# One more of the sixteen expert groups computed ahead: where the spilled products and the early picks stand, and the fourth one-hot buffer as one tensor

## What is computed

```python
def peer_ffn(xn, wq, keys, u_tab, v_tab):            # per token: 8 heads, 16 experts each
    q = (xb @ wq).reshape(C, PEER_HEADS, 2, PEER_DK_HALF)
    s = jnp.einsum('chpd,hpnd->chpn', q, keys)
    sv, si = lax.top_k(s, K)                         # K = 16, for both halves of the key
    cand = sv[:, :, 0, :, None] + sv[:, :, 1, None, :]
    cidx = si[:, :, 0, :, None] * N_KEYS + si[:, :, 1, None, :]
    top_s, sel = lax.top_k(cand.reshape(C, PEER_HEADS, K * K), K)
    eidx = jnp.take_along_axis(cidx.reshape(...), sel, axis=-1)
    g = jax.nn.softmax(top_s, axis=-1)
    act = jax.nn.gelu(jnp.einsum('chkd,cd->chk', u_tab[eidx], xb))
    return jnp.einsum('chk,chkd->cd', g * act, v_tab[eidx])
...
    h = h + peer_ffn(rmsnorm(h, g_ffn_norm[l]), peer_wq[l], peer_keys[l], peer_u[l], peer_v[l])
```

## Time and profile before

| | |
|---|---|
| Time, median of 3 runs | 2046.16 us (2044.97 to 2049.4) |
| Time of the profiled execution | 2044.4 us |
| Its span | 2042.6 us |
| PE busy | 1989.7 us (97%) |
| DVE busy | 1513.5 us (74%) |
| POOL busy | 1076.8 us (53%) |
| ACT busy | 980.6 us (48%) |
| DMA | 446.78 MB, mean 219 GB/s |
| Three scatter tiles | 424.8 to 707.7 us |
| Expert stage | 707.7 to about 1452 us |

### The profile page before, as it was taken

One profiled execution on the slowest core, in us unless ns is written; L12 is line 12 of the kernel. 1 busy time (PEld: TensorE's weight loads), 2 busy tenths in 40 slices (PEclk: granted clock), 3 DMA queues, 4 the chain that ended last, 5 costly groups with the idle time before them and its releaser, 6 DMA issues.

```text
span 2042.6 us, 31709 instructions
## 1 busy us (share of the span) xinstructions
PE 1989.7 (97%) x11783; PEld 1775.4 (87%) x11783; DVE 1513.5 (74%) x2883; ACT 980.6 (48%) x1805; POOL 1076.8 (53%) x646
## 2 busy tenths in 40 slices
PE   9999999999889999999999999999999999999998
PEld 8746889999889999999999999999877787877787
DVE  6237548989899858989999999988686635067763
ACT  4337433356779833333433333334556652255643
POOL 3213456875445767776777777674335444411242
PEclk9999999999899999999999999999999999999999
DMA  5330224767678999999999999997312222210021
GB/s 206 81 101 12 73 93 158 260 212 266 225 255 294 344 354 377 403 393 372 392 385 381 401 387 413 365 399 254 119 68 93 84 93 103 95 40 32 21 83 62
DMA packets 155144, 446.78 MB, mean 219 GB/s; under 512 B 14960, under 2 KB 60912, under 8 KB 152816
## 3 DMA queue, kind: packets, MB, share of 16 engines
q1 hardware_dynamic: 108912, 276.96, 38.4%
q0 software_dynamic: 46080, 167.79, 21.6%
HBM read 405.39 MB, written 39.31 MB: 218 GB/s over the span
## 4 chain that ended last, share of the span: by engine, by line
PE 77%; DVE 13%; DMA 3%; issue 3%; ACT 2%; POOL 2%; SPq 0%; DVEq 0%; ACTq 0%
PE bank L528 16%; PE bank L529 16%; PE bank L530 16%; PE bank L934 3%; PE bank L936 3%; PE bank L935 3%; PE bank L915 2%; PE bank L1156 2%; DVE fetched L2384 1%; PE bank L703 1%; DVE hots L2341 1%; DVE wide L2404 1%; DMA fetched<-in_v_rows,extra_rows 1%; PE wide L1179 1%; PE wide L1167 1%
## 5 line engine op out<-in xcount | busy, mean ns | idle before, releaser
L2725 POOL TENSOR_TENSOR wl<-wraw,wh 128x1024 fp32r<-128x1024 f32 x272 | 670.9, 2471 | 616.1 <-ACT wh L1347 613.9
L1347 ACT CAST wh<-wraw 128x1024 fp32r<-128x1024 f32 x360 | 374.1, 1045 | 150.5 <-PE bank L530 120.2
L528 PE MATMUL bank<-WTH,wh 128*128 128x352 f32 x1024 | 333.9, 326 | 7.6 <-issue 7.4
L529 PE MATMUL bank<-WTL,wh 128*128 128x352 f32 x1024 | 332.1, 324 | 0.0
L530 PE MATMUL bank<-WTH,wl 128*128 128x352 f32 x1024 | 332.0, 324 | 0.0
L528 PE MATMUL bank<-AXH,wh 128*128 128x352 f32 (+1 forms) x832 | 299.3, 360 | 6.9 <-issue 3.4
L530 PE MATMUL bank<-AXH,wl 128*128 128x352 f32 (+1 forms) x832 | 295.6, 355 | 0.0
L529 PE MATMUL bank<-AXL,wh 128*128 128x352 f32 (+1 forms) x832 | 295.5, 355 | 0.0
L934 PE MATMUL bank<-AXH,wh 128*128 128x352 f32 x576 | 193.7, 336 | 10.6 <-issue 10.6
L528 PEld LDWEIGHTS bank<-WTH,wh 128*128 128x128 f32 x1024 | 192.1, 188 | 12.7 <-issue 12.2
L2848 POOL DMA_INDIRECT fetched<-in_u_rows,diag x128 | 140.0, 1094 | 108.5 <-DVE fetched L2384 87.7
(11 more groups left out here) (557 smaller groups left out, 4116.2 us busy)
## 6 DMA issues: line engine op xcount, KB each, us to landing
wraw<-in_wstream SPq DMA_DIRECT2D x360, 512.0 KB
g_scratch<-gs SPq DMA_DIRECT2D x11, 2048.0 KB
gr<-g_scratch SPq DMA_DIRECT2D x15, 1408.0 KB
a_scratch<-tmp SPq DMA_DIRECT2D x72, 176.0 KB
tmp<-a_scratch SPq DMA_DIRECT2D x44, 176.0 KB
sq<-a_scratch SPq DMA_DIRECT2D x28, 176.0 KB
shifted<-hc_scratch SPq DMA_DIRECT2D x12, 270.0 KB, 4.8
h<-in_hT SPq DMA_DIRECT2D x8, 264.0 KB, 6.1
```

Of the source, the lines that this page charges most:

```text
L528: pe.matmul(o, w1, x1, start=n == 0, stop=False)
L529: pe.matmul(o, w1, x2, start=False, stop=False)
L1347: act.copy(wh[n % NSPLIT][:, :], wraw[n % NRAW][:, :]).then_inc(*w_hi.tell(n))
L2725: return pool.tensor_tensor(lo, src, hi.bitcast(F32), ALU.subtract)
```

## The change

One more group is spilled, so that its 8 U products leave the expert stage for the scatter tiles. The three tiles get 18, 20 and 12 spilled products for 15, 14 and 13, and 8, 12 and 26 early picks for 12, 12 and 22. The places of the six groups that stay dense are chosen anew. The two `sq` buffers become the halves of one tensor, so that the fourth one-hot pair is written by one DVE instruction in place of two. The weight stream is laid out in the new order.

```diff
-SPILLED = 9
-DENSE_AT = (0, 2, 4, 7, 9, 11, 14)
+SPILLED = 10
+DENSE_AT = (0, 2, 5, 8, 11, 14)
...
-    sq = [sb(ctx, f"sq{i}", [128, T]) for i in range(2)]
+    both_sq = sb(ctx, "sq", [128, 2, T])
+    sq = [both_sq[:, i, :] for i in range(2)]
...
-    hots.append((*(x[:, 0:512].rearrange("p (i c) -> p i c", i=4) for x in sq), None))
+    hot3 = both_sq[:, :, 0:512].rearrange("p a (i c) -> p a i c", i=4)
+    hots.append((hot3[:, 0, :, :], hot3[:, 1, :, :], hot3))
...
-                base, count = ((30, 15), (45, 14), (59, 13))[tt - 1]
+                base, count = ((30, 18), (48, 20), (68, 12))[tt - 1]
...
-                while picks < (10, 22, 34)[tt - 1] + (12, 12, 22)[tt - 1] * now // whole:
+                while picks < (10, 18, 30)[tt - 1] + (8, 12, 26)[tt - 1] * now // whole:
...
-                if q % 4 == 3:
-                    for x in range(2):
-                        dve.tensor_tensor(hots[3][x], iota_psum.unsqueeze(1).to_broadcast([128, 4, 128]),
-                                          places[:, x].to_broadcast([128, 4, 128]),
-                                          ALU.is_equal).then_inc(*hot.tell((q, x), q))
...
+                dve.tensor_tensor(hots[q % 4][2], iota_psum.unsqueeze(1).unsqueeze(1).to_broadcast([128, 2, 4, 128]),
+                                  places.to_broadcast([128, 2, 4, 128]), ALU.is_equal).then_inc(*hot.tell(q))
```

More of the change, by code:

```diff
@@ L2328, in scatter @@
                 places = ijgT[:, 0:2, 4 * q:4 * q + 4].unsqueeze(3)
-                if q % 4 == 3:
-                    for x in range(2):
-                        dve.tensor_tensor(hots[3][x], iota_psum.unsqueeze(1).to_broadcast([128, 4, 128]),
-                                          places[:, x].to_broadcast([128, 4, 128]),
-                                          ALU.is_equal).then_inc(*hot.tell((q, x), q))
[L2334 to L2342, removed]
+                if q == 33:
+                    dve.wait_ge(*ld_e.at("all"))
+                    dve.scalar_tensor_tensor(eidx2, shared[:, 0:EXTRA], 128.0, shared[:, EXTRA:2 * EXTRA], ALU.mult,
+                                             ALU.add).then_inc(*routed.tell((1, "experts")))
+                    dve.tensor_reduce(token_of, ident.rearrange("p (t a) -> p t a", a=SHARED), AX.X,
+                                      ALU.add).then_inc(*routed.tell((1, "token")))
+                dve.tensor_tensor(hots[q % 4][2], iota_psum.unsqueeze(1).unsqueeze(1).to_broadcast([128, 2, 4, 128]),
+                                  places.to_broadcast([128, 2, 4, 128]), ALU.is_equal).then_inc(*hot.tell(q))
         spilled = [0]
```

## The result

The changed kernel took 2064.68 us (median; 2061.79 to 2067.16) against 2045.57 of the kernel before on the same chip: ratio 1.009, 95% interval 1.0071 to 1.0108. It is 19 us slower where I forecast 4.7 faster, and lies outside my range.

The account below looks back on a forecast made before the run. PE, busy 97% of the span, was taken as the bound, with DVE tighter in crowded stretches. Scatter tiles +18 and expert stage -22.7 gave -4.7 us: 2041.5 us for the median, own range 2033 to 2048, 8 in 10 2029 to 2053.

Parts of the forecast that it names:

- Tile 3: Third scatter tile: one product fewer, four picks more, set by DVE; +5 us, between -4 and +7.
- the new layout of the products: Third scatter tile: one product fewer, nothing in the sum as DVE sets the tile; -4 us if PE alone did.
- Dense stretches: Expert stage: 2.4 us more DVE work in each, hidden behind PE; length left at 64.0 us, five of them.
- rival 1: Expert stage: DMA bytes set it, 603 us for 611.7; kernel 9.4 us slower, 2055.6 us; chance 0.16.
- Crowded stretches: Expert stage: 1.1 picks more in each, DVE the tighter engine; 32.5 to 33.6 us, eight of them.
- The ceiling of 358 GB/s: Expert stage: HBM limit giving 664 us before and a loss of 10 us overall; rejected because rows show 390 GB/s.
- Tile 1: First scatter tile: three products more, four picks fewer, the wait for `ijg` gone; +1 us, between 0 and +4.
- Tile 2: Second scatter tile: six products more, half-clock stretch gone, PE sets it; 114 us, +12, between +10 and +17.
- Rest of the stage: Expert stage outside stretches 1 to 13: stretch 0 gets one pick more, last stretches keep theirs; 0 us.
- a change of PE's pace: Expert stage: a shift between 3.8 and 4.0 us a product, no cause seen; 0.2 us over 144 products, 29 us.

Follow-up runs that it names:

- e3: The kernel before with only the early picks changed, to 8, 12 and 26: 2057.41 us, ratio 1.0054, third tile 102.2 us.
- e15: The changed kernel with gate stores from block 7 on at a quarter of their bytes, the rest filled early: 2069.75 us, third tile 98.6 us.
- e17: As e15, with 16 weight tiles of the third scatter tile also loading 128 of 1024 columns: 2063.88 us, third tile 95.2 us.
- e1: The changed kernel with the old early picks, 12, 12 and 22: 2053.64 us, ratio 1.0026, third tile 96.0 us.
- e9: The changed kernel with half the columns of weight tiles loaded in stretches 1 to 13: 2046.67 us, ratio 1.0, these stretches 580.5 us.
- e10: The changed kernel with later picks over 768 of 1024 columns on DVE: 2050.88 us, ratio 1.0016, stretches 1 to 13 588.1 us.
- e7: The changed kernel with POOL fetching early picks' rows two picks ahead, not three: 2066.97 us, ratio 1.0097, third tile 110.0 us.

## Why the prediction was wrong

- **Tile 3, "I take +5", bounds -4 and +7: the step that failed most.** It costed four picks by their time on DVE and took DVE's wait for rows as it stood, 5.5 us. Measured: +18. The wait grew to 19.4 us, it passed through ACT and POOL to PE, 13 us of idling, and PE's clock fell with its three gaps, about 6 us more. e3 shows the step alone: +15 with nothing but the picks changed; e15 and e17 show that the wait follows the DMA engines' load. A row that could have warned me was the window of tile 3, with a DMA share of 0.95. A second term stood in the sum as nothing, and as -4 in its lower bound: the new layout of the products. With the old picks it made the tile 9 us longer (e1).
- **Dense stretches, "2.4 us more for DVE ... Hidden behind PE; I leave 64.0": the second.** DVE's part was nearly right (busy 58.4 for 55.2, +3.2). But each pick also brings a row of 0.52 MB, and each dense stretch got two rows more (30.6 fetches for 28.7, by their times). By the windows a stretch moved 24.4 MB (62.6 us at 390 GB/s) and now 25.8 (65.6 at 394). Measured +2.9 each, 15 us in five. e9 shows it: with the bytes gone, 62.5. It is the sign that I had given for rival 1, dense stretches beyond 65 us with longer waits for `fetched` (31.6 us in the stage for 20.0).
- **Crowded stretches, +1.1 each, to 33.6: the rise was too much.** By one cut they were 33.6 before and 33.7 after: they got 0.5 picks more each (11.4 for 10.9, by their times) and not 1.1, the rest went to the dense ones. DVE sets them as I said (busy 32.55 of 33.7; e10). That the length of 33.6 came true is luck: the start of 32.5 was a matter of the cut, and the rise did not come.
- **Rival 1** (DMA sets the stage, decides below 396 GB/s) had 0.16. The mean was 394, on its side of the bound, and its mechanism holds for the dense stretches alone; the stage lost 13.5 us, between its 8.6 and my 22.7. What I held against it, that a crowded stretch's length doesn't follow the rate, was true and told nothing of the dense ones. The ceiling of 358 GB/s that the Trainium skill names (DMA: Bandwidth & Descriptors, "Where 436 GB/s comes from") doesn't hold here either: 394 over 597 us.
- **Tile 1, +1: measured +4**, my upper bound. DVE should have fallen from 86.6 to 80 us with four picks fewer, and stayed at 86.5, so the wait for `ijg` stayed (4.1 us for 7.9). Groups of DVE in tile 1, before and then after, show why:
```profile
L2384 DVE SCALAR_TENSOR_TENSOR fetched<-fetched,below_XH 128x1024 f32<-128x1024 f32 x13 | 22.1, 1707 | 0.0
...
L2293 DVE TENSOR_TENSOR spare<-selu,sie 128x2048 uint32<-128x2048 uint32 x2 | 4.6, 2286 | 0.0
```
```profile
L2380 DVE SCALAR_TENSOR_TENSOR fetched<-fetched,below_XH 128x1024 f32<-128x1024 f32 x9 | 19.3, 2147 | 0.0
...
L2295 DVE TENSOR_TENSOR spare<-selu,sie 128x2048 uint32<-128x2048 uint32 x2 | 6.6, 3308 | 0.0
```
  A pick took 1707 ns on average and takes 2147. POOL had three splits more in this tile. e3, which moves the picks and leaves the splits, bears this out: DVE busy 80.3 us, as forecast, and 1671 ns a pick.
- **Tile 2, +12: measured +11**, with PE busy 112.5 of 112.6 us. Its clock was 0.98 and not 1.00: a wait for `ijg` of 4.1 us was left, and the 3.4 us at half clock begin where it ends, at 522.5 us.
- **Rest of the stage, nothing: measured +4**, of it 3 us in stretch 14 (37.2 us for 34.1). Other runs of the same stage took 33.3 to 36.9 us there, so this need not be the change's doing.

What was to upset the sum altogether, a change of PE's pace, did not come: PE was busy 3.95 us a product in stretches 1 to 13 (568.8 / 144), as before (601.6 / 152).

## What to carry to other kernels

Cost a moved or added gather by its bytes as well as by its compute time, and look at how busy the DMA engines are where it goes (here a share of 0.95 before, and 390 GB/s in the dense stretches): engines that run their lists in order hand a late transfer on, here from DVE to ACT, POOL and PE. A stage made of two kinds of stretch needs a bound for each kind; one mean hides that one is set by bytes and the other by an engine. And asking for a row later, to free the engine that waits to ask (e7), only moved the wait to the next engine.

## What the runs showed of the hardware

- A DVE operation with two inputs in SBUF and a POOL split don't run side by side. Of the early picks of both kernels in the scatter tiles, set beside POOL's splits by their times, 46 overlapped with no split and took 1.21 to 1.29 us. Of the other 46, 37 took 1.09 us plus the overlap, to within 0.06: 1.52 us with 0.43 of it, 2.50 with 1.41, 3.32 with 2.23. Of the other nine, three took 1.21 us, and the split beside them 3.3 to 3.5 us for 2.4; the last six waited for one split, and five of the next splits took 3.4 us. The Trainium skill (SBUF — State Buffer, "🔬 SBUF: two separate sides") says that the two engines take turns on a shared pair of ports under an exclusive lock; this trace agrees.
- A gap of PE cost more than its length: with each of the three gaps of 2.7, 5.2 and 6.5 us in tile 3 came 3.4 to 6.9 us at half clock, in which PE was busy 11.2 us: about 6 us lost beside 13 us of added idling.
- Waits for gathered rows fall faster than the bytes beside them: in e15 6 of the tile's 31 MB were gone (251 GB/s for 295), in 6144 packets of 1 KB of 15774 in all, and DVE's waits for rows fell by 14 of 19.4 us. Whether it is the bytes or the number of packets no run here separates.
